# Transposing and scaling in one matmul: diagonal matrices of reciprocal roots instead of a normalising pass

## The reference

```
def rmsnorm(x, g):
    xf = x.astype(jnp.float32)
    y = xf * lax.rsqrt(jnp.mean(xf * xf, axis=-1, keepdims=True) + RMS_EPS)
    return (y * g.astype(jnp.float32)).astype(x.dtype)

h = h + 0.5 * swiglu(rmsnorm(h, ffn1_norm[layer]), w_gate, w_up, w_down)     # ffn0, ffn2
hn = rmsnorm(h, mix_norm[layer])                                             # mix_a, mix_b
h = h + mixer(hn, ...)
h = h + 0.5 * swiglu(rmsnorm(h, ffn2_norm[layer]), w_gate, w_up, w_down)     # ffn1, ffn3
k, v = (rmsnorm(h, kv_norm) @ kv_w)                                          # kv
```

## Time and profile before

| | |
|---|---|
| median of 3 runs | 2717.62 us (2714.75 to 2731.52) |
| the profiled execution | 2725.85 us, of which the span of the core is 2724.0 us |
| TensorE busy | 2435.3 us, 89% of the span |
| VectorE, ScalarE, GpSimd busy | 1423.4, 716.3 and 885.6 us |
| moved by DMA | 690.72 MB, mean 254 GB/s |

### The profile page before, as it was taken

The page is one execution under the profiler, slowest core; times in us unless marked ns, Lnnn a source line. Parts: engine busy times, 40 slices in busy tenths (PEclk is TensorE's granted clock), DMA queues, the critical chain, the costliest instruction groups (busy, mean ns, idle before and its releaser), DMA issues. The chain is left out here.

```text
span 2724.0 us, 40823 instructions
## 1 busy us (share of the span) xinstructions
PE 2435.3 (89%) x16128; PEld 1718.8 (63%) x16128; DVE 1423.4 (52%) x1965; ACT 716.3 (26%) x1022; POOL 885.6 (33%) x530
## 2 busy tenths in 40 slices
PE   7999889999998899899977988998788978898885
PEld 6997779988997799845864433333276753343332
DVE  7876579766886589644655222222266452222213
ACT  4333433334333433212111111111144321111111
POOL 6888888848885088111330000000000000000000
PEclk9998889999998899889998999999988779999998
DMA  7775347655664166443013999999933149999995
GB/s 291 251 254 203 140 158 250 250 192 202 247 246 178 63 247 246 162 133 135 4 36 141 419 419 421 421 422 422 374 131 124 44 169 421 420 421 421 422 421 224
DMA packets 110151, 690.72 MB, mean 254 GB/s; under 512 B 15744, under 2 KB 17088, under 8 KB 35152
## 3 DMA queue, kind: packets, MB, share of 16 engines
q1 hardware_dynamic: 88704, 618.10, 58.0%
q0 software_dynamic: 20320, 70.85, 7.4%
q10 hardware_dynamic: 1008, 0.06, 0.0%
HBM read 687.85 MB, written 1.11 MB: 253 GB/s over the span
## 5 line engine op out<-in xcount | busy, mean ns | idle before, releaser
L694 PE MATMUL bank<-ring,B 128*64 128x512 f32 (+1 forms) x3264 | 787.8, 603 | 100.3 <-DMA ring<-in_moe_wgate 66.1
L1932 DVE TENSOR_TENSOR ring_r<-ring,B_r 128x2048 fp32r<-128x2048 f32 x184 | 544.1, 2975 | 195.4 <-ACT B_r L1497 195.1
L694 PEld LDWEIGHTS bank<-ring,B 128*64 128x64 f32 (+1 forms) x3264 | 270.9, 141 | 575.3 <-issue 558.3
L694 PE MATMUL bank<-B_r 128*128 128x512 f32 (+1 forms) x1992 | 533.8, 353 | 13.4 <-DVE B L2195 5.3
L1497 ACT ACTIVATE B_r<-ring 128x2048 fp32r<-128x2048 f32 x184 | 346.8, 1909 | 291.7 <-PE bank L694 289.5
L694 PEld LDWEIGHTS bank<-B_r 128*128 128x128 f32 x1992 | 344.8, 193 | 109.7 <-issue 56.8
L694 PE MATMUL bank<-xt_r,B_r 128*128 128x256 f32 x1408 | 400.0, 284 | 11.9 <-DVE ring_r L1932 8.3
L694 PE MATMUL bank<-xt_r,ring_r 128*128 128x256 f32 x1408 | 398.7, 283 | 0.0
L694 PEld LDWEIGHTS bank<-xt_r,B_r 128*128 128x128 f32 x1408 | 269.9, 192 | 14.7 <-issue 11.1
L694 PEld LDWEIGHTS bank<-xt_r,ring_r 128*128 128x128 f32 x1408 | 270.0, 192 | 0.0
L2703 POOL TENSOR_TENSOR wkx<-wkx,small_s 128x1024 f32<-128x1024 f32 x84 | 206.3, 2465 | 72.9 <-DMA wkx<-in_ada_w 61.9
(11 more groups left out here) (350 smaller groups left out, 3066.0 us busy)
## 6 DMA issues: line engine op xcount, KB each, us to landing
ring<-in_moe_wgate SPq DMA_DIRECT2D x128, 1024.0 KB, 8.5
ring<-in_moe_wup SPq DMA_DIRECT2D x128, 1024.0 KB, 8.7
ring<-in_moe_wdown SPq DMA_DIRECT2D x128, 1024.0 KB, 9.7
ring<-in_ffn_w_gate SPq DMA_DIRECT2D x44, 1024.0 KB, 4.9
ring<-in_ffn_w_up SPq DMA_DIRECT2D x44, 1024.0 KB, 5.0
ring<-in_ffn_w_down SPq DMA_DIRECT2D x44, 1024.0 KB, 5.0
wkx<-in_ada_w POOLq DMA_DIRECT2D x72, 512.0 KB, 6.2
B<-in_ada_w POOLq DMA_DIRECT2D x24, 512.0 KB, 8.8
```

The lines of the kernel that those rows point to most:

```text
L694: ins = pe.matmul(out, lhsT, rhs, start=start, stop=stop, skip_group_check=True)
L1932: dve.tensor_tensor(ring_r[:, slot, :], ring[:, slot, :], f32(hi), ALU.subtract).then_inc(sp_lo, 1)
```

## The change

The pass that multiplies the tokens goes. VectorE instead multiplies the 128x128 identity by the reciprocals of each half, which gives two diagonal matrices; they lie in the first 256 columns of `Xn`. TensorE then runs an ordinary fp32 matmul with a block of raw `X` as the stationary operand and the diagonal matrix as the moving one: the product is the block transposed, each column scaled by its token's reciprocal root. ScalarE no longer takes part, and its semaphore `nm_act` goes. `ffn2` uses the two matrices that were made for `kv`. All other transposes (`mix_r` and those of attention and the experts) stay as they were. At the very start VectorE waits for the identity before it normalises, not behind it.

```
+        diag = [Xn[:, 0, h * P:(h + 1) * P] for h in range(TB)]
...
-                if name in NORMED:
-                    pe.wait_ge(nm_act, NORMED.index(name) + 1)
+                scaled = name in NORMED or name == "ffn2"
...
-                            x = src[:, h, k * P:(k + 1) * P]
+                            x = (X if scaled else src)[:, h, k * P:(k + 1) * P]
...
-                            mm(tr_bank(name, b)[:, c:c + P], x, ident, transpose=True,
+                            mm(tr_bank(name, b)[:, c:c + P], x, diag[h] if scaled else ident, transpose=not scaled,
                                signal=tr_pe if k % 2 and h else None)
...
-                if n < len(NORMED):
-                    act.wait_ge(nm_inv, n + 1)
-                    act.activation(Xn[:, 1, :], X[:, 1, :], ACT.Copy, scale=rms_i[n % 2][:, 1:2]).then_inc(nm_act, 1)
...
-                dve.tensor_scalar(Xn[:, 0, :], X[:, 0, :], rms_i[n % 2][:, 0:1], None, ALU.mult).then_inc(tr_src, 1)
+                for h in range(TB):
+                    ins = dve.tensor_scalar(diag[h], ident, rms_i[n % 2][:, h:h + 1], None, ALU.mult)
+                ins.then_inc(tr_src, 1)
...
+            dve.wait_ge(in_landed, 48)
             normalise(0, "ffn0")
```

More of the change, by code:

```diff
@@ L392, in build @@
         nm_inv = sem("nm_inv")
-        nm_act = sem("nm_act")
         row_landed = [sem(f"row_landed{i}") for i in range(NROW)]
```

## The result

The changed kernel takes 2737.47 us (median of 20 runs, 2727.32 to 2760.86) against 2725.57 us for the kernel before in the same session (20 runs, 2714.28 to 2737.74). The ratio on record is 1.006, with a 95% interval of 1.0042 to 1.0079; it isn't the quotient of the two medians, which is 1.0044, and the means of the same runs differ by 13.9 us. So it is slower by 0.6%, within the 1% that the prediction called no change, and inside its range; but the interval is 11 to 21 us, where the sum had +5. Against the 2725.57 us here that sum would be 2730.6. To lie inside the range took some luck: over all its 38 runs in three sessions the changed kernel has a mean of 2743.4 us, above the upper end of 2741. The profiled execution took 2736.63 us, its span 2734.8.

A forecast was written before the change was run, and what follows sets the result against it. TensorE, busy 89% of the span, was taken as the bound. Start gains, dearer matmuls and clock credits summed to +5.0 us: 2725.85 becomes 2731, and with the median 8.2 us lower the forecast is 2722.6 us, range 2708 to 2741.

The forecast's parts named there:

- the sum: Gains and costs added over the seven transposing places of the first trunk: +5.0 us for the kernel.
- what is added: At seven places 16 matmuls, each costing two transposes; from half clock 5.5 us against 3.65, +1.85.
- what the clock gives back: Products behind the matmuls start at full clock: 1.9 us won at `mix_a`, 1.5 at `mix_b`, 0.5 at `ffn1`.
- the long end: At places starting at half clock, 4 us of dense work bring the clock back: 18 of 32 records done by then.
- the credit for products at the full clock: Time won in the products at `mix_a` (1.9 us), `mix_b` (1.5) and `ffn1` (0.5); none at `kv`.
- the starts: TensorE starts 0.47 us behind the reciprocals, not 1.20: 0.73 won at `ffn0`, `mix_a`, `ffn1`, `ffn3`, 2.9 us in all.
- The clock stays at half: Rival: half clock lasts through the matmuls at the cold places; +18 us, 2735.6; chance 0.17.
- The clock comes back at once: Rival: the 16 matmuls at a place take 3.5 us, at full clock almost immediately; -9 us, 2709; chance 0.13.
- Load and stream don't overlap: Rival: each matmul record pays weight load and stream, 0.22 or 0.44 us; 2747 or 2781 us; chance 0.10.

The follow-up runs named there:

- the seven traces with matmuls: Changed kernel three times (1.006, 1.0105, 1.0056); kernel before with matmuls against the identity twice (1.0061, 1.004); changed kernel with diagonals on ScalarE twice (1.0036, 1.0061).
- the five traces with single transposes: Kernel before three times (repeats 0.9991, 1.0004); kernel before with scaling left out of the transposes (0.9991); kernel before with the pass in pieces (1.0005).
- the matmuls alone: Kernel before with its pass kept, ordinary fp32 matmuls against the identity in place of transposes at seven places, run twice: 2737.6 us (1.0061), 2739.39 us (1.004).
- the first repetition of before: The kernel before run again unchanged, for a further trace: 2723.68 us, ratio 0.9991.
- the first repetition of after: The changed kernel run again unchanged, for a second trace: 2756.05 us, ratio 1.0105 from six runs.
- Doubled transposes: Kernel before with each of the 16 transposes at the seven places issued twice: 2735.57 us, ratio 1.003.

## Why the prediction had the right kind of cost and too little of it

**What held.** A matmul is two records and costs two transposes: 224 records, 32 to a place, and doubled they cost what the full clock asks. TensorE starts 0.54 us behind the scaling at `ffn3` in all three traces of after and at `ffn1` in two (forecast 0.5, and a gain of 0.66 for 0.73). The clock comes back inside the row, and every product of `mix_a`, `ffn1`, `kv` and `mix_b` starts at 1.00: in all 28 cases of the seven traces with matmuls, against 8 of the 20 in the five traces with single transposes. `ffn1` has its 7.02 us, forecast 7.0, in the first trace; in the other two it is longer by what VectorE's small instructions are held up, but so it is in the other two of before, and from the reciprocals to the product the means are 8.72 and 7.68 us: +1.0, forecast +1.1. `ffn2` hides its longer row: its product starts 11.09 us behind the first transpose, before 10.98. `ffn3` is +1.7 at the product, as forecast (by its own row the old transposes ended at 943.2, not 943.0, so the sum should have had +1.5).

**The step that failed is the sum's "what is added" with what the clock gives back**: +8 us for the matmuls alone, where the runs show +14.4 (4.5 either way). The sum followed each place only up to the start of its product and took the rest of the stage as unchanged; more than half of what it missed lies there. It came apart in five terms. Time from the first transposing record to the first matmul of the product, three traces of each kernel:

| place | before | after | longer by | forecast |
|---|---|---|---|---|
| `ffn0` | 10.25, 10.26, 10.25 | 13.15, 12.60, 13.03 | 2.7 | 1.85 |
| `mix_a` | 4.67, 4.59, 4.66 | 6.25, 6.29, 6.84 | 1.8 | 1.85 |
| `ffn1` | 4.69, 5.94, 5.92 | 6.48, 7.75, 6.42 | 1.4 | 1.85 |
| `kv` | 4.66, 4.61, 4.67 | 7.17, 7.61, 6.92 | 2.6 | 1.85 |
| `mix_b` | 4.67, 5.21, 4.59 | 7.02, 7.33, 7.49 | 2.5 | 1.85 |
| `ffn3` | 10.05, 10.47, 10.52 | 12.72, 12.81, 12.71 | 2.4 | 2.4 |

First, the clock came back later than the 4 us that I called the long end: in the twelve rows of `mix_a` to `mix_b` in the three traces of after, 3.0 to 6.1 us were at half clock, 4.5 on average. The 32 records took 5.2 to 6.7 us, 5.9 on average, not 5.5, and the places grew by 13.4 us where 11.7 were booked: +2.

Second, the credit for products at the full clock, 3.9 us, was read from one execution, and the places were not the right ones. In its trace `mix_a` and `mix_b` started at half clock; in the first repetition of before `mix_a` started at the full clock already. And the faster product meets VectorE. Stretches of 3.8 us from the start of the product at `mix_a` and of 3 us at `mix_b`, in the first repetition of before and in after, to be laid beside the earlier trace rows:

```profile
223.60:227.40 3.80, 3.78 (x16) 3.10 (x17) 3.76 (x9) 0.05 (x1) 3.51 (x2) 1.00 0.87 328
847.80:850.80 3.00, 3.00 (x7) 2.39 (x8) 3.00 (x8) 0.00 (x0) 2.82 (x3) 0.50 0.00 0
```
```profile
228.40:232.20 3.80, 3.80 (x16) 3.08 (x17) 3.80 (x9) 0.00 (x0) 2.91 (x4) 1.00 0.59 166
859.00:862.00 3.00, 3.00 (x13) 2.45 (x14) 2.98 (x8) 0.00 (x0) 2.82 (x2) 1.00 0.00 0
```

TensorE is through 16 matmuls instead of 9, and 13 instead of 7, so the clock is real; but VectorE is full in all four, among others with the weight splits that the later matmuls need. At `mix_a` of the first repetition of after, the next split was caught behind GpSimd and TensorE waited:

```profile
229.83 2.41 POOL L2706 TENSOR_TENSOR wkx<-wkx 128x1024 f32<-128x1024 f32 x1 [0.18 <-POOL wkx L2702]
230.07 4.32 DVE L1930 TENSOR_TENSOR ring_r<-ring,B_r 128x2048 fp32r<-128x2048 f32 x1
...
234.53 0.47 PE L694 MATMUL bank<-B_r,xt_r 128*128 128x512 f32 x1 [1.78 <-DVE ring_r L1930]
```

From the start of the product to its 32nd matmul, five traces with single transposes took 8.01 to 9.51 us at `mix_a`, mean 8.9, and three of after 7.34, 9.33 and 8.65, mean 8.4; at `mix_b` 8.5 and 7.5. So 0.5 and 1.0 us came back of 1.9 and 1.5: -1.5 for -3.4. At `ffn1` the 0.5 came back as forecast: up to the end of the 32nd matmul it took 4.97 to 4.99 us in all seven traces with matmuls and 5.43 on average in the five with single transposes. And at `kv`, which got no credit because its product started at the full clock in the one trace read, it did so in only two of those five; 8.9 us became 7.7, -1.2. In all -3.1 came back of -3.9: +0.8. The same argument, VectorE full whatever the clock, I had used for `ffn1`; the earlier trace rows had it for `mix_a` and `mix_b` too, with 3.80 of 3.80 and 3.00 of 3.00.

Third, the feed-forward behind `ffn3`. The stage up to `mix_r` grew by 4.2 us on average, in the traces with 16 matmuls, and is steady (202.2 to 204.1 against 205.5 to 208.6), where +2.3 stand at the start of the product, by the same averages. The other 1.9 us are added inside the product, and the traces show where. Some 33 us into it TensorE waits for a weight split of VectorE. First before, then after, with the stretch that follows there:

```profile
984.62 0.39 PE L694 MATMUL bank<-xt_r,B_r 128*128 128x256 f32 x1 [0.94 <-DVE ring_r L1932]
```
```profile
1006.83 0.58 PE L694 MATMUL bank<-xt_r,B_r 128*128 128x256 f32 x1 [2.00 <-DVE ring_r L1930]
...
1006.70:1010.10 3.40, 3.27 (x15) 3.27 (x16) 3.33 (x5) 0.00 (x0) 2.09 (x3) 0.51 0.00 0
```

In five of the seven traces with matmuls this wait is 1.88 to 2.00 us, 3.4 us at 0.50 follow, and from the start of the product to the reciprocals of `mix_r` they take 194.5 to 194.6 us. In the other two it is 0.72 and 0.92, the clock stays up, and they take 191.8 and 191.9. With single transposes the wait is 0 to 1.97 us, the clock stays up even behind the longest, and the five traces take 190.4 to 193.0. So about 1 us is the wait and 1.7 the clock. Doubled transposes, with a wait of 1.97 and no fall, take 192.9. What makes the wait longer was not tried. +1.9.

Fourth, the feed-forward behind `ffn2`, where the sum had +0.2 for the whole place. Its product came 1.5 us sooner behind the 32nd matmul of `kv` (49.8 us for 51.3), but from its start to the reciprocals of `mix_b` the traces with matmuls took 197.3 us on average and those with single transposes 193.6: +3.7. Of this 3.0 lie between the last matmul of that product and the reciprocals, where VectorE's small instructions of the norm are held up. At `mix_b`, in the kernel before and in the first repetition of after:

```profile
832.71 0.16 DVE L1885 TENSOR_TENSOR small_s<-small_s 128x2 f32<-128x2 f32 x1
832.90 0.17 DVE L1886 TENSOR_SCALAR small_s<-small_s 128x2 f32<-128x2 f32 x1
```
```profile
846.27 2.34 POOL L2702 TENSOR_TENSOR wkx<-wkx,small_s 128x1024 f32<-128x1024 f32 x1
...
846.90 1.72 DVE L1881 TENSOR_TENSOR small_s<-small_s 128x2 f32<-128x2 f32 x1
848.57 1.89 POOL L2702 TENSOR_TENSOR B<-B,small_s 128x1024 f32<-128x1024 f32 x1
848.66 1.82 DVE L1882 TENSOR_SCALAR small_s<-small_s 128x2 f32<-128x2 f32 x1
```

That end of the stage took 2.3 to 6.0 us in the five traces with single transposes and 5.6 to 8.8 in the seven with matmuls, and 8.5 with doubled transposes. The instructions are the same in all: they only come later, and beside GpSimd's. So it seems to be the lateness, and not the new instruction, that costs here; no run was made to show it.

Fifth, the starts. From the reciprocals to the first transposing record the six places gained 1.65 us together (three traces of each kernel), not 2.9: `ffn0` and `ffn3` 0.6 to 0.7 each, `ffn1` 0.3 and `mix_a` nothing on average, since the diagonals were held up there in one trace of three. +1.3.

This makes 5.0 + 2 for the rows + 0.8 for the credits + 1.9 for `ffn3` + 3.7 - 1.5 - 0.2 for `ffn2` + 1.3 for the starts = 13 us. The stages of the traces show +14.6, 8 either way, and the runs +16.4, 3.6 either way, or +15.4, 1.9 either way, at equal clock. What is left, 2 to 3 us, is near the errors and has no place in any row.

**The rivals.** *The clock stays at half* gave 2735.6, near the measured time, but every trace contradicts its reason. *The clock comes back at once* falls: each of the twelve rows above has 3.0 us or more at 0.50. *Load and stream don't overlap* falls: 0.11 a record, no row over 6.8 us. With it goes the price of four to one that the Trainium skill has for fp32 ("TensorE: Matmul & The Clock Gate", Terms): this kernel shows two to one. The rule of the Trainium skill to do logical transposes as transposes ("Perfetto Trace Analysis", Transposes) was right here, by 14.4 us, 4.5 either way.

## What to carry to other kernels

Folding a pass into TensorE trades time of two idle engines for time of the one that is the bound: count its records (two for an fp32 matmul, one for a transpose) before the pass that goes, and if it is the wait at the start that hurts, cut the pass in pieces instead. A credit for a faster clock is worth only what the engine beside leaves of it, and it is read from several executions, not from one. A sum that ends where the product starts leaves out what a late product meets further on. When two traces differ in stages whose code is the same, run the old kernel again before explaining anything, and compare runs at equal clock too.

## What the runs showed of the hardware

- The time at half clock differs from execution to execution of one kernel. In the first expert layer it is 738.9 x (1 - 0.93) x 2 = 103 us of 738.9, or 724.9 x (1 - 0.95) x 2 = 72 us of 724.9; half of the difference, some 15 us, is about the difference in length, 14.0. It is the size of the whole effect of the change.
- The clock comes back from 0.50 while TensorE runs nothing but fp32 transposes: within 32 of them in 5.57 us (0.50, 0.91, then 1.00), and within 16 in 3.44 us behind 10.3 us of idleness. In the five traces with single transposes it was back by the start of the product in 8 of 20 cases.
- A small VectorE instruction can last far longer beside a GpSimd one: 0.24 us became 1.91 and 1.93 for two of 128 columns, which ended 0.08 us behind the GpSimd instructions beside them, and 0.16 became 2.22 for one of 2 columns. ScalarE's two in their place took 0.69 us, and TensorE started 0.95 us behind the reciprocals in all eight cases. Small is no protection.
